# Three scheduling edits in a streaming encoder step: weight low parts on VectorE, spills issued by ScalarE, and TensorE's dense unit ahead of its attention share

## The reference, cut to what matters

```python
x = x + 0.5 * SwiGLU_1(RMSNorm(x))
z = RMSNorm(x) @ w_in
A = differential attention, 4 heads, q and k in two 64-wide halves, values 128 wide, per-head RMSNorm
B = sparse attention, 8 query heads, one key and one value head; a 4-head indexer picks 256 keys per query
x = x + concat(A, B) @ w_out
x = x + 0.5 * SwiGLU_2(RMSNorm(x))       # D_MODEL 1024, D_FF 2816
```

## Time and profile before

| | |
|---|---|
| median of 3 runs | 3033.25 us (3026.32 to 3037.68) |
| the profiled execution | 3029.14 us |
| its span, first to last instruction | 3027.1 us, mean granted TensorE clock 0.917 |
| busy: TensorE / VectorE / ScalarE / GpSimd | 86% / 45% / 28% / 10% |
| DMA | 222 MB, 73 GB/s over the span |

### The profile page before, as it was taken

The page is one execution under the profiler, slowest core; times in us unless marked ns, Lnnn a source line. Parts: engine busy times, 40 slices in busy tenths (PEclk is TensorE's granted clock), DMA queues, the critical chain, the costliest instruction groups (busy, mean ns, idle before and its releaser), DMA issues. The chain is left out here.

```text
span 3027.1 us, 35924 instructions
## 1 busy us (share of the span) xinstructions
PE 2596.3 (86%) x13666; PEld 2285.3 (75%) x13666; DVE 1369.9 (45%) x2671; ACT 857.7 (28%) x1431; POOL 311.8 (10%) x260
## 2 busy tenths in 40 slices
PE   5999999999988996357795868888889977999998
PEld 4999999999976885246664856666767756988988
DVE  5333333333343323486432578876555323443343
ACT  3111111111122111354212455543333213222221
POOL 1000000000012120010001223333212100000000
PEclk8999999999998998567897879999989987999999
DMA  5111111111012213411633512322221132221220
GB/s 187 42 42 42 42 42 42 42 42 42 0 35 87 106 43 122 150 42 32 183 103 113 135 49 74 92 82 71 57 66 52 47 133 91 83 73 52 83 83 35
DMA packets 197715, 222.02 MB, mean 73 GB/s; under 512 B 29393, under 2 KB 158193, under 8 KB 196721
## 3 DMA queue, kind: packets, MB, share of 16 engines
q1 hardware_dynamic: 197616, 220.78, 23.0%
HBM read 177.79 MB, written 32.74 MB: 70 GB/s over the span
## 5 line engine op out<-in xcount | busy, mean ns | idle before, releaser
L506 PE MATMUL a_bank<-XTh_a,f_gu_hi 128*128 128x384 f32 x1056 | 353.7, 335 | 3.0 <-DVEq L487 3.0
L507 PE MATMUL a_bank<-XTl_a,f_gu_hi 128*128 128x384 f32 x1056 | 353.5, 335 | 0.0
L508 PE MATMUL a_bank<-XTh_a,f_gu_lo 128*128 128x384 f32 x1056 | 353.4, 335 | 0.0
L471 DVE TENSOR_TENSOR f_hid<-f_silu,a_bank 128x384 f32<-128x384 f32 x66 | 36.6, 554 | 420.4 <-ACT f_silu L443 420.4
L1850 POOL TENSOR_TENSOR h_w_lo<-h_w_raw,h_w_hi 128x2048 fp32r<-128x2048 f32 x37 | 170.6, 4611 | 501.4 <-ACT h_w_hi L2064 501.4
L506 PE MATMUL b_bank<-XTh_b,f_gu_hi 128*128 128x320 f32 x704 | 218.9, 311 | 3.0 <-DVEq L487 3.0
L507 PE MATMUL b_bank<-XTl_b,f_gu_hi 128*128 128x320 f32 x704 | 218.7, 311 | 0.0
L508 PE MATMUL b_bank<-XTh_b,f_gu_lo 128*128 128x320 f32 x704 | 218.6, 311 | 0.0
L506 PEld LDWEIGHTS a_bank<-XTh_a,f_gu_hi 128*128 128x128 f32 x1056 | 198.7, 188 | 3.8 <-DVEq L487 3.4
L507 PEld LDWEIGHTS a_bank<-XTl_a,f_gu_hi 128*128 128x128 f32 x1056 | 198.8, 188 | 0.4
L508 PEld LDWEIGHTS a_bank<-XTh_a,f_gu_lo 128*128 128x128 f32 x1056 | 198.8, 188 | 0.0
(11 more groups left out here) (393 smaller groups left out, 5711.5 us busy)
## 6 DMA issues: line engine op xcount, KB each, us to landing
f_gu_raw<-in_w_gate SPq DMA_DIRECT2D x22, 1024.0 KB, 5.4
f_gu_raw<-in_w_up SPq DMA_DIRECT2D x22, 1024.0 KB, 7.9
f_d_raw<-in_w_down SPq DMA_DIRECT2D x22, 1024.0 KB, 5.4
h_w_raw<-in_w_gate SPq DMA_DIRECT2D x22, 512.0 KB, 4.0
h_w_raw<-in_w_up SPq DMA_DIRECT2D x22, 512.0 KB, 5.3
h_w_raw<-in_w_down SPq DMA_DIRECT2D x11, 1024.0 KB, 5.1
win_w_raw<-in_w_in SPq DMA_DIRECT2D x4, 2048.0 KB, 8.5
s_k_in<-in_cache_diff_k SPq DMA_DIRECT2D x8, 1024.0 KB, 5.4
```

Source lines behind the costliest of these rows:

```text
L471: dve.tensor_tensor(hid[:, n % 2], silu[:, n % 2], psum[2 * (n % 2) + 1][:, 0:TOK_CHUNK], ALU.mult).then_inc(gated, 1)
L506: pe.matmul(out, hi, XTh[:, k, tok], start=(k == 0), stop=False)
L507: pe.matmul(out, hi, XTl[:, k, tok], start=False, stop=False)
L508: last = pe.matmul(out, lo, XTh[:, k, tok], start=False, stop=(k == KD - 1))
```

## The change

Five edits, in `early_attention` and `late_half`:

1. The four spills are issued by ScalarE, ahead of its first instruction of the block, and no longer by SyncE.
2. `split_lo` goes from GpSimd to VectorE, one step later, behind `take` and ahead of the marking and of `attend(k)`.
3. The last two operations of `norm_head` go from GpSimd to VectorE as one operation, in the odd step of pass a where a - 5 was the mixing pass (GpSimd's two small ones stay at a - 4).
4. SyncE stores a head (or row of heads) one pass later (a - 6 for a - 5).
5. TensorE does `dense(k)` ahead of `attend(k)`.

```diff
@@ early_attention, sync
                 load(0)
                 load(1)
-                for dst, src in spills:
-                    sp.dma_start(dst, src).then_inc(spilled, 16)
                 sp.dma_start(dv[:, 0:NP], ...)
@@ early_attention, scalar
             def _(act):
+                for dst, src in spills:
+                    act.dma_start(dst, src).then_inc(spilled, 16)
@@ late_half, sync
-                    if sub == 1 and a - 5 in head_mixed_at:
-                        store(head_mixed_at[a - 5])
+                    if sub == 1 and a - 6 in head_mixed_at:
+                        store(head_mixed_at[a - 6])
@@ late_half, gpsimd
-                def split_lo(c):
-                    pool.wait_ge(hi_split, c + 1)
-                    pool.tensor_tensor(w_lo[:, c % 2], w_raw[:, c % 2], w_hi.bitcast(F32)[:, c % 2], ALU.subtract
-                                       ).then_inc(lo_split, 1)
...
-                    pool.wait_ge(orstd_ready, j + 1)
-                    pool.tensor_scalar(o, o, orstd[:, j:j + 1], None, ALU.mult).then_inc(oscaled, 1)
-                    pool.wait_ge(oscaled, j + 1)
-                    pool.tensor_tensor(o, o, sub_gain[:], ALU.mult).then_inc(onormed, 1)
...
-                    for c in range(N_CHUNKS):
-                        if split_step(c) == k:
-                            split_lo(c)
@@ late_half, tensor
                 for k in range(STEPS):
-                    attend(k)
                     if k < N_UNITS:
                         dense(k)
+                    attend(k)
@@ late_half, vector
-                    elif a in head_mixed_at:
-                        mix(head_mixed_at[a])
+                    else:
+                        if a in head_mixed_at:
+                            mix(head_mixed_at[a])
+                        if a - 5 in head_mixed_at and head_mixed_at[a - 5] < n_diff:
+                            norm_head(head_mixed_at[a - 5])
+
+                def norm_head(j):
+                    o = o_ring[:, j % 8, :]
+                    dve.wait_ge(orstd_ready, j + 1)
+                    dve.scalar_tensor_tensor(o, o, orstd[:, j:j + 1], sub_gain[:], ALU.mult, ALU.mult).then_inc(onormed, 1)
+
+                def split_lo(c):
+                    dve.wait_ge(hi_split, c + 1)
+                    dve.tensor_tensor(w_lo[:, c % 2], w_raw[:, c % 2], w_hi.bitcast(F32)[:, c % 2], ALU.subtract
+                                      ).then_inc(lo_split, 1)
...
                         take(u)
+                    for c in range(N_CHUNKS):
+                        if split_step(c) + 1 == k:
+                            split_lo(c)
```

More of the change, by code:

```diff
@@ L1681, in late_half @@
         orstd_ready = sem("h_orstd_ready")
-        oscaled = sem("h_oscaled")
         onormed = sem("h_onormed")
@@ L1859, in norm_head @@
                 def norm_head(j):
-                    o = o_ring[:, j % 8, :]
                     pool.wait_ge(osquared, j + 1)
```

## The result

| | before | after |
|---|---|---|
| median (range) of 4 runs each | 3030.94 us (3026.32 to 3037.68) | 3077.84 us (3077.59 to 3078.47) |
| ratio, 95% interval | | 1.0153 [1.0133, 1.0174] |
| span and mean clock of the profiled execution | 3027.1 us, 0.917 | 3076.7 us, 0.915 |

A forecast was written before the change was run, and what follows sets the result against it. TensorE was taken to bound the merged block's pairs, with VectorE also near its bound in the search pairs. +10 + 19 - 4 + 2 + 2 - 2 = +27 on 3029.1 gave 3056, forecast as 3060 us; range 3016 to 3091.

The forecast's parts named there:

- GpSimd's split: Merged block: 4578 ns, 37 times; each split meeting a VectorE SBUF-only operation costs VectorE some 4 us; all that goes.
- The split on VectorE: Odd steps between `maximum` and `mix`: 2.5 us each by the slope, 37 times, 92 us; +7.5 us in a pair.
- the normalisation: One 128 x 128 VectorE operation in odd steps: 16 x 0.3 = 5 us, hidden by TensorE's share.
- Group B: Five later pairs of the merged block: floor + 8.3 us idle + 3.4 for two cold units each; sum +10 us.
- The search pairs: Four merged-block pairs that carry the search: 64 us against 59, +4.8 each, +19 us together.
- The other eight units: Units outside the down group in a search pair: 37 us before, 34 after, by fewer locks and more splits.
- The head of the block: Units 20 to 23 wait for scaled rows, some 1.5 us more each, less one lock: +2, ends 0 and +8.
- Settling pair, last pair, last store: Pair 2006 to 2071 with VectorE's settling: -4 us; final pair without maxima: 0; final store a pass later: +2.
- Spills: Early attention's head: small copies wait for DMA engines, not SyncE; -2 us, ends -22 and +3.
- Clock: Rival, chance 0.15: reopened waits stay warm, no cold unit in nine pairs, 31 us less: 3029 us.
- Copies that pass: Rival, chance 0.08: in the early attention the small copies pass the spills, 18 us off, 3042 us.
- VectorE's returned time sets the pace: Rival, chance 0.14: without locks the four search pairs take 51 us each, not 64; -52 us, giving 3008.

## Why the prediction came out as it did

- **GpSimd's split.** Right. The 128 x 256 operation is at 0.42, and the edit alone gives 56 us. What the prediction did not say is how little of that would remain behind the new waits (19), and that most of it lies in group B.
- **The split on VectorE**: 2.28 us measured for 2.5 by the slope, 84 us for 92; the normalisation 0.35 for 0.3. Right, and not in the way.
- **Group B.** The five pairs took 57.2, 62.2, 62.1, 61.9 and 65.1 us for 60, 61, 63, 64 and 66. Floor plus three idles plus two cold units was the right sum: there were ten cold units in the five pairs, though three of them at r = 8 and only two at r = 9. The experiments agree on the mechanism: with earlier drains the five pairs take 262.6 us, with the old order in the down units 266.2, for 308.5.
- **The search pairs** hold the miss: 69.4 us for 64, four times: 21.5 us, of the 22.6 by which the spans' difference exceeds the forecast's (the misses of the other pieces nearly cancel). The down group was nearly right (29.4, 33.0, 29.7 and 31.9 us for 29.8). The term that missed is "The other eight units: 37 before, now 2 x 4 us of locks less and 2 x 2.5 of splits more: 34". They took 38.4 in the mean. The subtraction itself was sound: with the same splits and the old order they take 34.7. The new order puts 3.7 on top, and 3.6 of it lie in one place, from the end of unit r = 7 to the start of r = 8: 8.0 us in the mean against 4.4. I had priced the chain there at 2.3 us, by its own operations and for group B, and had nothing for it here. In these pairs a maximum and a round stand ahead of its product on VectorE, and counts and an exponential ahead of its copy on ScalarE; the wait was 5.1 to 7.6 us. The runs with the rounds moved bear it out: with no round near r = 8 the fourth pair's wait falls from 5.86 us to 1.98, as in group B, and in the kernel with earlier drains from 6.56 to 0.27. Rounds ahead of the maximum take only a part of it away (from unit 7's end to unit 8's start 6.3 us for 8.0).
- **The head of the block**: +8.9 against +2, just past the bound of +8. The waits of units 20 to 23 were priced about right: 2.36, 5.97, 5.45 and 3.77 us where before they were 1.66, 8.30, 4.18 and 1.75, 1.7 more in sum. What the sum left out is the first gate unit, which waits for the last of these drains: 5.09 us for 1.35. The other 3.8 us have gone before unit 20 starts; no run takes them apart. That the drains' place sets this stretch, and not the rounds' place within a step, the runs show: from the block's first transpose to the first gate unit the kernel before takes 131.0 us, the kernel after 139.8, the one with earlier drains 125.2, the one with rounds first 138.6. How many rounds stand there counts too, as the moved rounds showed. The timeline of TensorE before, unit 21 and the first gate unit:

```profile
1752.12 1.97 PE L1922 MATMUL h_result<-ident,h_rows 128*128 128x128 f32 x8 [8.30 <-DVE h_rows L2220]
...
1769.15 0.47 PE L1939 MATMUL h_gate<-h_XTh,h_w_hi 128*128 128x512 f32 x1 [1.35 <-DVE h_XTl L2184]
```

  And after:

```profile
1755.09 1.97 PE L1908 MATMUL h_result<-ident,h_rows 128*128 128x128 f32 x8 [5.97 <-DVE h_rows L2206]
...
1777.44 0.77 PE L1925 MATMUL h_gate<-h_XTh,h_w_hi 128*128 128x512 f32 x1 [5.09 <-DVE h_XTl L2170]
```

- **Settling pair, last pair, last store**: -1.1 for -4, -3.0 for 0, 0 for +2: small, and 2 us less together than forecast.
- **Spills**: the -2 was right in size. TensorE's first scores came 3 us sooner and DMA stayed the limit (the DMA engines are busy at 0.87 or more through the wait, 1212 to 1232 us of the kernel after). SyncE's block on sv did go (1.35 us for 11.51), and it issued the first copy 7.6 us after the block's start for 17.1, but the data came only those 3 us sooner. The query rows even came later with ScalarE's spills beside them: TensorE's first transposes began 6.0 us after the block's start for 2.2 (1210.08 - 1204.04 and 1204.90 - 1202.74). The clause "even if it blocked for those 11.5 us it would stay inside the 29" wasn't put to the test by this change, in which ScalarE's four issues took 3.2 us. With sv on its queue it did block, for 12.00 us, the high part of the queries moved with it, and the first scores came at 30.6 us, 1.4 later than after. So a block does reach TensorE there; with nothing ahead of the copies and ScalarE free the first scores came at 23.7.
  By the Trainium skill (DMA: Bandwidth & Descriptors, "Issuing engines are not separate DMA queues") DMAs of several issuers run on the same engines and only issue time is saved. That gave about 0 for this term, and the totals agree: no kernel in which only queues differed was measurably faster.
- **Rivals.** Clock: it did not stay warm; cold excess doubled. Copies that pass: 3 us, not 18. VectorE's returned time sets the pace: false under the new order, but with the splits alone, under the old order, the search pairs came down to 60.6, 55.0, 52.2 and 54.5 us, towards its 51. The rival was right that the locks hold these pairs up, but had their share wrong: the four gave 15 us where 59 to 51 would be 32, and group B, where it had nothing, gave 33. And it was wrong that TensorE's new order lets this time be used.

## What to carry to other kernels

When two streams are interleaved on one engine, swap their order only together with the order in which the other engines take the results: in an in-order program a drain that stands behind a read of something later costs wherever the next unit needs that drain at once. Here that is 66 to 101 us in all, 91 of the 101 in four steps of twelve. Price a chain by what stands ahead of each link in each engine's program, not by its links. And look at bundled edits one by one: the one that gains (56 us) was hidden behind the one that costs.

## What the runs showed that I had not expected

- Gains don't add. The same edit was worth 56 and 19 us, by TensorE's order.
- 2.80 us of idle time at r = 9 was followed by a warm unit and 2.71 at r = 11, in the same group, by a cold one. The stretches in the columns of the earlier trace rows:

```profile
2356.00:2361.00 5.00, 4.62 (x15) 3.68 (x15) 1.68 (x4) 1.01 (x2) 0.00 (x0) 0.66 0.00 0
2344.00:2348.00 4.00, 3.35 (x17) 2.83 (x18) 3.96 (x5) 1.24 (x2) 0.00 (x0) 1.00 0.00 0
```

  The length of one idle stretch doesn't settle which level the next unit gets (0.66 against 1.00 in the mean); no run here says what does.
- An engine that issues a DMA behind the 9 MB of spills and dv on its own queue stands still: 12.00 us on ScalarE, as 11.51 on SyncE.
